# Two-layer hybrid decoder trunk: gMLP's v product first, norms by token halves, gate products one branch ahead, and the order of the last expert blocks

## The reference

```
h = rmsnorm(x, attn_norm_gain)
q, k, v, pz, gu, gv, g = split(h @ w_in)
gates = sigmoid(g + b_gate)                       # 3 branches x 1024
ya = sliding_window_attention(q, k, v, sinks, rel_bias) @ w_branch_a
yb = multiscale_pool(pz, w_pool, pool_scale) @ w_branch_b
yc = (gelu(gu) * spatial(rmsnorm(gelu(gv), v_gain))) @ w_branch_c
x = x + (gates[0]*ya + gates[1]*yb + gates[2]*yc) @ w_out
h2 = rmsnorm(x, ffn_norm_gain)
x = x + peer(h2)      # 8 heads, product keys, top 16 of 128*128 experts, gelu(h2 @ u) * gate @ v
```

## Time and profile before

| | us |
|---|---|
| median of 3 runs | 2060.33 |
| lowest and highest | 2059.02, 2060.73 |
| the profiled execution | 2059.37 |
| its span | 2057.6 |
| TensorE busy in it | 2017.3 |

### The profile page before, as it was taken

The page is one execution under the profiler, slowest core; times in us unless marked ns, Lnnn a source line. Parts: engine busy times, 40 slices in busy tenths (PEclk is TensorE's granted clock), DMA queues, the critical chain, the costliest instruction groups (busy, mean ns, idle before and its releaser), DMA issues.

```text
span 2057.6 us, 41405 instructions
## 1 busy us (share of the span) xinstructions
PE 2017.3 (98%) x13730; PEld 1874.1 (91%) x13730; DVE 1469.7 (71%) x2984; ACT 1057.9 (51%) x1751; POOL 1028.4 (50%) x427
## 2 busy tenths in 40 slices
PE   7999999999999999999989999999999999999997
PEld 6999899999998888889889999999999988888896
DVE  3943169688887888886649341796888778888775
ACT  5644454577774333334365444546777733333343
POOL 5798679877770000004368886797777600000042
PEclk9999999999999999999999999999999999999999
DMA  7455557665667777876454554576565677787763
GB/s 260 135 185 185 173 180 228 223 199 194 196 198 227 242 240 241 242 242 218 162 186 144 187 188 169 187 229 217 195 199 195 195 238 241 241 242 240 233 215 122
DMA packets 164486, 423.36 MB, mean 206 GB/s; under 512 B 18075, under 2 KB 76620, under 8 KB 163868
## 3 DMA queue, kind: packets, MB, share of 16 engines
q1 hardware_dynamic: 163724, 418.24, 63.3%
...
...
## 4 chain that ended last, share of the span: by engine, by line
PE 93%; issue 2%; POOL 2%; ACT 1%; DVE 1%; DMA 0%; DVEq 0%; POOLq 0%; ACTq 0%
PE bank L1112 53%; PE bank L1313 34%; PE bank L1364 3%; POOL halves L463 2%; PE bank L1291 1%; DVE hT L792 0%; PE bank L1274 0%; PE bank L1134 0%; PE bank L1213 0%; ACT area L505 0%; DMA x<-in_x 0%; ACT halves L528 0%; DVE area L785 0%; ACT area L559 0%; PE bank L1223 0%
## 5 line engine op out<-in xcount | busy, mean ns | idle before, releaser
L463 POOL TENSOR_TENSOR halves<-ring,halves 128x1024 fp32r<-128x1024 f32 x412 | 1021.8, 2490 | 992.7 <-DVE coef L1045 617.7
L528 ACT ACTIVATE halves<-ring 128x1024 fp32r<-128x1024 f32 x668 | 705.3, 1057 | 759.5 <-PE bank L1313 408.2
L1112 PE MATMUL bank<-hT,halves 128*128 128x256 f32 x8736 | 1081.5, 283 | 10.2 <-DVE hT L792 9.3
L1112 PEld LDWEIGHTS bank<-hT,halves 128*128 128x128 f32 x8736 | 1063.8, 192 | 16.2 <-DVE hT L792 10.8
L1313 PE MATMUL bank<-halves,coef 128*128 128x512 f32 x3072 | 703.0, 389 | 0.0
L1313 PEld LDWEIGHTS bank<-halves,coef 128*128 128x128 f32 x3072 | 574.4, 188 | 118.6 <-issue 0.5
L1027 DVE TENSOR_TENSOR halves<-ring,halves 128x1024 fp32r<-128x1024 f32 x256 | 315.8, 1234 | 10.4 <-ACT halves L528 10.0
L1039 DVE TENSOR_TENSOR act<-act,area 128x256 f32<-128x256 f32 x256 | 157.5, 615 | 58.8 <-ACT act L641 55.8
L1043 DVE CAST coef<-act 128x256 fp32r<-128x256 f32 x256 | 75.4, 294 | 100.8 <-PE bank L1313 98.0
L690 ACT ACTIVATE onehot<-onehot,weight 128x128 fp32r<-128x128 f32 x256 | 89.1, 395 | 108.2 <-DVE onehot L1010 108.1
L1004 DVE TENSOR_TENSOR onehot<-bank,ids 128x512 fp32r<-128x512 f32 x128 | 88.6, 692 | 48.5 <-PE bank L1364 48.5
...
## 6 DMA issues: line engine op xcount, KB each, us to landing
...
area<-rel_scratch SPq DMA_DIRECT2D x2, 1024.0 KB, 6.2
x_home<-x ACTq DMA_DIRECT2D x2, 1024.0 KB, 4.2
x<-x_home SPq DMA_DIRECT2D x2, 1024.0 KB, 8.0
rel_scratch<-act POOLq DMA_DIRECT2D x1, 1532.0 KB, 14.7
...
```

The lines of the kernel that those rows point to most:

```text
L463: pool.tensor_tensor(halves[:, s, 1, :], ring[:, s, :], halves[:, s, 0, :].bitcast(F32), ALU.subtract)\
L528: a.activation(halves[:, s, 0, :], ring[:, s, :], ACT.Copy).then_inc(hi_done, 1)
L1112: i = pe.matmul(o, stationary[a], moving[b], start=begin and n == 0, stop=end and n == len(TERMS) - 1)
```

## The change

Six things are done together.

1. The entry of a layer. x comes in two token halves on two queues; the parameters (`par`) come by a transfer of their own and not by the stream; SyncE, and no longer GpSimd, writes the relative bias rows out. The norm is made for one token half (`normed`): VectorE writes x times root times gain, TensorE transposes that against the identity, ScalarE and VectorE take high and low sides from PSUM. At layer 0 two matmuls spread the gain row over the partitions.
2. gMLP's v product, four tiles, follows the norm directly and goes by token halves; its gelu, root and scaling follow it. The triangle product of GpSimd now stands behind the low side of tile 19.
3. The four gate tiles of branch n + 1 come ahead of the two tiles of branch n (`MIX`), those of branch 0 before the attention transposes.
4. The output projection finishes token half 0 first, and the second norm goes by halves. Five matmuls that nothing reads (`KEEPERS`) replace four identity matmuls of 512 columns.
5. The last u block of a layer moves ahead of v block 125, and the last three v blocks go by token halves, so that half 0 is added to x and normed while half 1 is multiplied.
6. The final norm goes by halves with a gain that was loaded before, and the output is written in four transfers. Banks are allotted anew for this order.

```diff
+MIX = [("gate", 0)] + [step for n in range(2 * BR - 1) for step in (("gate", n + 1), ("branch", n))] + [("branch", 2 * BR - 1)]
+T_GATE, T_BRANCH = ([T_MIX + sum(4 if kind == "gate" else 2 for kind, _ in MIX[:MIX.index((name, n))])
+                     for n in range(2 * BR)] for name in ("gate", "branch"))
...
+    + [("lg1", "V")] * 4 + [("pz", "V")] * 2 + [("gu", "A")] * 2 + [("gate", "A")] * 2
+    + [("pT0", "A")] * 2 + [("pT1", "A")] * 4 + [("attn", "A")] * 4 + [("gmlp", "V")] * 2 + [("pool", "V")] * 2
+    + [(kind, "A" if kind == "gate" else "V") for kind, _ in MIX[1:] for _ in range(2)]
+    + [("wo", "V")] * 3 + [("h2T", "V")] * 2 + [("wo", "V")] + [("h2T", "V")] * 2 + [("qq", "A")] * 8 + [("score", "A")] * 8
...
+                if l == 0:
+                    sp.dma_start(x[:, 0, :], x_in[0, 0:P, :]).then_inc(x_loaded[0], 16)
+                    load(2, 2, l)
+                    sp.dma_start(ids[:, :], consts_in[:, 0:2 * P]).then_inc(consts_loaded, 16)
+                    load(3, 3, l)
+                    sp.dma_start(oh, consts_in[0:BUCKETS + 1, K_OH:K_END]).then_inc(rel_loaded, 16)
+                    sp.dma_start(relx[0:BUCKETS, :], rel_in).then_inc(rel_loaded, 16)
+                    load(4, 0, l)
+                    load(5, 1, l)
+                    sp.wait_ge(rel_vector, 1)
+                    sp.dma_start(scratch.rearrange("h (r i) d -> (h r) i d", i=HEADS),
+                                 relv.unsqueeze(1).to_broadcast([P, HEADS, NDIST])).then_inc(rel_written, 16)
...
+                for s in range(2, RING):
                     sp.wait_ge(lo_pool, l * LOP + (s + 2))
                     load(RING + s, s, l)
+                if l == 0:
+                    for s in range(2):
+                        sp.wait_ge(lo_pool, l * LOP + RING + s + 2)
+                        load(2 * RING + s, s, l)
                 sp.wait_ge(rel_written, 16)
                 sp.dma_start(bias, bass.AP(scratch.tensor, P - 1, [[NDIST - 1, P], [P * NDIST, HEADS], [1, 2 * P]]))\
                     .then_inc(bias_loaded, 16)
-                with sp.Fori(2, T_PU // RING + 1) as r:
-                    for s in range(RING):
+                if l == 0:
+                    load_maps(l)
+                def load_early(r, begin=0):
...
             for l in range(DEPTH):
 
-                pool.wait_ge(params_ready, l + 1)
+                pool.wait_ge(hi_done, l * HIS + 1)
                 pool.sem_inc(lo_pool, 2)
-                low(2, 2, l)
+                subtract(2)
                 low(3, 3, l)
-
+                with pool.Fori(1, 5) as r:
+                    for s in range(RING):
+                        low(r * RING + s, s, l)
+
+                pool.wait_ge(params_loaded, l * 16 + 16)
                 pool.wait_ge(maps_loaded, l * 16 + 16)
                 for g in range(GROUPS):
                     i = pool.tensor_tensor(wsp[:, g, :], par[:, C_WSP + g * P:C_WSP + (g + 1) * P], tril, ALU.mult)
                 i.then_inc(wsp_ready, 1)
-                with pool.Fori(1, T_PV // RING) as r:
+                with pool.Fori(5, T_PV // RING) as r:
                     for s in range(RING):
...
+                def gates(n):
+
+                    if n >= 3:
+                        a.wait_ge(taken_v, l * NGV + taken_before(place("branch", 2 * (n - 2) + 1) + 1)[0])
+                    for k in range(2):
+                        high_up_to(T_GATE[n] + 2 * k + 1 + 3)
+                        b = group("gate")
+                        for c in range(2):
+                            hf, br = divmod(n, BR)
+                            col = C_BGATE + br * KD + hf * 4 + 2 * k + c
+                            i = a.activation(sig_of(n)[:, 2 * k + c, :], b[:, c * S:(c + 1) * S], ACT.Sigmoid,
+                                             bias=par[:, col:col + 1])
+                        i.then_inc(taken_a, 1)
+
+                gates(0)
                 for n in range(2):
                     b = group("pT0")
...
+                def normed(n, t, gain):
+                    rstd(n + t, 2 + t, 4 + t, 1)
+                    for c, cols in enumerate(COLS):
+                        v.scalar_tensor_tensor(hn[:, t, cols], x[:, t, cols], stat[:, 4 + t:5 + t], gain(c),
+                                               ALU.mult, ALU.mult).then_inc(hn_ready, 1)
+
...
+                def gate_rows(j, t):
+
+                    if j % 2 == 0:
+                        pe.wait_ge(taken_v, rows_ready("h1T", 2 * t + j // 2 + 1))
+                    w = tile(T_GV + j, 2)
+                    for k in range(2):
+                        rows = [hT[:, e, 2 * j + k, t * P:(t + 1) * P] for e in range(2)]
+                        one, i = product(bv[t][:, :], rows, (w[:, 0, k], w[:, 1, k]), j == 0 and k == 0, j == 3 and k == 1)
+                        if t == 1 and k == 0:
+                            one.then_inc(tiles_used, 1)
+                    if j == 3:
+                        i.then_inc(groups_done, 1)
+
+                gate_rows(0, 0)
+                gate_rows(1, 0)
+                transpose_rows("h1T", 0, 1)
+                gate_rows(2, 0)
+                for j in range(3):
+                    gate_rows(j, 1)
+                gate_rows(3, 0)
+                gate_rows(3, 1)
...
-                            if t == 0 and k == 0:
-                                one.then_inc(tiles_used, 1)
-                        if kq == 3:
-                            i.then_inc(groups_done, 1)
-
-                pe.wait_ge(taken_v, l * NGV + taken_before(first("h2T"))[0])
-                for t in range(TT):
-                    for hf in range(2):
-                        pe.matmul(acc[2 * t + hf][:, :], ident, x[:, t, hf * HALF_N:(hf + 1) * HALF_N], start=True,
-                                  stop=True)
-                pe.wait_ge(diag_ready, l * 2 + 2)
-                transpose_rows("h2T")
-                pe.wait_ge(scaled, l * 4 + 3)
+                        projected(n, t, t == 0)
+                pe.wait_ge(merged_ready, l * 4 + 4)
+                for n in range(4, 8):
+                    tile(T_WO + n, 2)
+                    projected(n, 0, n == 4)
+                for n in range(4, 7):
+                    projected(n, 1, n > 4)
+                transpose_rows("h2T", 4, 0)
+                projected(7, 1, True)
+                for n in range(KEEPERS):
+                    pe.matmul(bank[7][:, 0:S], ident, ids[:, :], start=True, stop=True)
+                transpose_rows("h2T", 4, 1)
+                g[0] = first("qq")
...
+                def v_half(s, factors, t):
+
+                    for a, e in TERMS:
+                        for hf in range(2):
+                            i = pe.matmul(acc[2 * t + hf][:, :], factors[:, a, t * P:(t + 1) * P],
+                                          halves[:, s, e, hf * HALF_N:(hf + 1) * HALF_N], start=False, stop=True,
+                                          skip_group_check=True)
+                    return i
+
+                pe.wait_ge(lo_vector, l * LOV + NK - 1)
+                pe.wait_ge(coef_ready, l * NK + NK - 2)
+                v_half(0, coef[:, 1], 0)
+                pe.wait_ge(lo_pool, l * LOP + (NK - 1) + (T_PV - EARLY + 2))
+                pe.wait_ge(coef_ready, l * NK + NK - 1)
+                v_half(1, coef[:, 0], 0)
+                pe.wait_ge(lo_vector, l * LOV + NK + 1)
+                pe.wait_ge(coef_ready, l * NK + NK)
+                v_half(3, coef_last, 0).then_inc(acc_done, 1)
+                v_half(3, coef_last, 1).then_inc(tiles_used, 1)
+                v_half(0, coef[:, 1], 1).then_inc(tiles_used, 1)
+                v_half(1, coef[:, 0], 1).then_inc(tiles_used, 1)
 
```

605 lines of the change are left out of this document (341 added, 264 removed).

## The result

The changed kernel takes **2080.78 us** (median of 4, 2077.42 to 2083.48) against 2059.82 for the kernel before (2059.02 to 2060.73): 1.0101 times as long, 95% interval 1.0083 to 1.0118. Forecast was 2059.5, between 2050 and 2066. In the profiled executions the span went from 2057.6 to 2079.2 us, so there are 21.6 us to account for.

A forecast was written before the change was run, and what follows sets the result against it. TensorE, busy 2017.3 of 2057.6 us, was taken to bound the kernel. Terms 3.4 + 9.5 + 2.8 + 1.4 - 5.9 - 10.4 = 0.8 gave 2058.6, stated as a 2059.5 median, range 2050 to 2066.

The forecast's parts named there:

- GpSimd before the first gates: Behind the logits: moved triangle products and earlier exponentials add 3.0 us of wait a layer, 5.9 lost for two layers.
- The second norm: Projection to query columns: 8.1 us lost in place of 9.5, a gain of 1.4 a layer, 2.8 in all.
- merged wait: Fifth projection tile: TensorE newly waits 1.9 us for all four merged pieces.
- rival (c): Slower: the clock falls in the new waits, 13 us more at most, half giving 2066; chance 0.04.
- rival (b): Slower: VectorE's norm pieces collide with low sides, 13 us at most, half giving 2066; chance 0.09.
- The entry: Kernel start: halved x gains 2.9 us, less 1.5 of queue waits, so a gain of 1.4, bounds -4 and 4.
- queue waits: Entry, SyncE's queue: bias write and parameters ahead of tile loads cost 1.5 us, up to 6.
- bias write: Entry: 1532 KB written from SyncE's queue, taking 7.6 us without added waits, or 14.7 as in the kernel before.
- The gates: Gates 3, 4 and 5: ScalarE's wait for the sig slot delays tiles by 1.7 to 1.9 us, 5.2 lost a layer.
- From layer to layer: Boundary between layers: 5.1 us lost in place of 14.6, a gain of 9.5, bounds 7 and 11.
- the wait for tile 4: Between layers: tile 4's high side comes only behind half 1's root, a new TensorE wait of 1.4 us.
- The end: After TensorE's last product: 8.0 us in place of 11.4, a gain of 3.4, bounds 3 and 4.5.

The follow-up runs named there:

- Experiment 2: Changed kernel with GpSimd waiting for the second maxima before the low side of tile 15: 2080.72 us, ratio 1.0097 to the kernel before.
- 4: Changed kernel with high sides up to tiles 16 and 18 ahead of the exponentials and triangle products behind tile 23: 2064.56 us, 1.0022 to the kernel before.
- 1: Changed kernel with high sides of tiles 15 to 18, not only 15 and 16, made before the second exponentials: 2079.17 us, 1.0094 to the kernel before.
- 3: Changed kernel with high sides up to tiles 16 and 18 ahead of the two blocks of exponentials, as before: 2076.35 us, 1.0079 to the kernel before.
- 5: Changed kernel with only the triangle products moved, behind the low side of tile 23: 2080.67 us, 1.0100 to the kernel before.
- 8: Changed kernel with the last four projection tiles reordered, each waiting only for its own part of merged: 2076.08 us, 1.0073 to the kernel before.
- experiment 9: Changed kernel with the third query tile's high side made behind token half 1's transposed rows: 2075.02 us, 1.0073 to the kernel before.
- experiment 7: Changed kernel with SyncE's layer 0 queue reordered: tile 6 before the bias write, parameters and maps behind tiles 10 and 11: 2078.99 us, 1.0095 to the kernel before.

## Why the prediction was wrong

**What failed: "GpSimd before the first gates", 2.95 a layer where 8.2 was measured.** The step priced the triangle products at 2.63 and the earlier exponentials at 1.5 and took off what GpSimd had in hand. It had seen that the second exponentials begin ahead of a high side, but it treated that as delay on one engine. What it lacked is the return path: GpSimd's idleness ahead of the exponentials puts its next low sides on VectorE's second maxima, those hold up the exponentials, and these hold up the high sides that GpSimd needs. Experiment 2 shows the first link, 4 that undoing both moves gives all 8.9 back, and 1, 2, 3 and 5 that working on one delay alone gives 0.6 to 3.8. Of the 8.9 in layer 0, 7.0 are waits (5.65 and 1.31), 1.6 is the slow clock behind the first (10.50 for 8.89), the rest restarts. Nor does the sum of two prices hold for two delays in a row on one engine: 0.8 and 3.4 apart, 8.9 together.

**"The second norm", a gain of 1.4 where 2.2 was lost, in each layer.** The merged wait was foreseen and came as 2.51 for 1.9. In layer 0, 33.7 stand against the forecast's 21.95 + 8.1 = 30.1. Of the 3.6 between them 0.6 is the merged wait; 1.6 is a slow clock behind it (42 products in 11.43, in layer 1 in 9.86), rival (c); and the chain behind the last half tile took 241.20 - 234.52 = 6.7 for 5.2, since the second piece of half 1's norm met the third query tile's low side, rival (b). Experiments 8 and 9 take away the first and the last. In layer 1 the clock stayed up, and in place of the 1.6 stand 1.30 of waiting on half 0's norm, whose second piece met the first query tile's low side. VectorE and GpSimd, first in layer 0, then in layer 1:

```profile
230.57 1.42 DVE L919 SCALAR_TENSOR_TENSOR area<-x,stat,area 128x512 f32<-128x512 f32 x2
231.28 5.29 POOL L526 TENSOR_TENSOR halves<-ring,halves 128x1024 fp32r<-128x1024 f32 x2 [6.14 <-ACT halves L608]
```

```profile
1255.55 3.62 DVE L919 SCALAR_TENSOR_TENSOR area<-x,stat,area 128x512 f32<-128x512 f32 x2
1256.24 5.18 POOL L526 TENSOR_TENSOR halves<-ring,halves 128x1024 fp32r<-128x1024 f32 x2 [4.54 <-ACT halves L608]
```

The low side begins 0.71 after the first piece in the one and 0.69 in the other, just where the second piece begins; for half 1, late in both layers, it is 0.68. So a few hundredths of a microsecond seem to decide whether that piece takes 0.7 or 2.9; no experiment moved them alone.

**"The entry", a gain of 1.4 where 2.2 was lost.** The queue waits were put at 1.5 and are 3.2 (experiment 7), inside their bound of 6. The bias write took 11.2 from issue to landing, between the 7.6 and the 14.7 of the working. The rest is the other half of the term: without these waits the entry wins 1.0 and not 2.9. Of that, 1.3 is that v starts at 15.69 and not at 14.4: its first low side is ready at 14.76, and the bias product (1.64) stands in between. Behind that the working foresaw 2 us of waiting for tile 4; TensorE has no idle row there, but v's first twelve products took 5.40, where twelve took 3.06 in layer 1, at a granted clock of 1.00 in both, and no run shows why. By the Trainium skill (page "SBUF — State Buffer", section "SBUF: two separate sides"), as the prediction read it, a write from SyncE's queue is not held up by VectorE, and the prediction put it near 7.6. The trace does not decide it: the write took 11.2, and four ring tiles shared the DMA engines with it.

**What held.** The gates: 4.4 of waits and 5.3 in all a layer for 5.2, at gates 3, 4 and 5, at the second tile, behind VectorE's taking; gate 4 was no worse than the others, since the halving stands behind the taking. From layer to layer: 9.7 for 9.5, v 2.6 after the last v block's end for 2.65, the wait for tile 4 1.32 for 1.4. The end: half 1's adds begin at 2072.37, 0.5 behind TensorE's last product (2069.09 + 12 x 0.2275), and the span ends 7.4 after that product, a gain of 4.0 for 3.4; the last row of the table shows 1.2 less, since it also holds 1.0 of slow clock behind the norm of layer 1; experiment 9, without it, has 810.37 there for 811.38.

**The rivals.** (b) and (c) had 0.09 and 0.04 and were priced as ends of their own. Both happened in part, on top of the forecast terms: 1.3 for half 1's piece in each layer and 1.3 for half 0's in layer 1, 1.6 and 2.0 for the clock at tile 17 (72 products in 10.50 and 10.90), 1.6 at the norm of layer 0. Against (b) the prediction said that ScalarE has only just begun the high side then. That was so each time: it began 0.42 to 0.44 ahead of the first piece. But a high side takes 1.06, and the second piece begins 0.7 behind the first, so the low side arrives just with the second piece; the argument covers the first one only. Of the port of VectorE and GpSimd the Trainium skill (page "SBUF — State Buffer", section "SBUF: two separate sides") says that the engine that starts first has it for the whole instruction and the other blocks fully. The traces agree: a piece is 0.7 or 2.9, an operation on 8 columns 0.17 or, just behind the start of a low side, 2.0 to 2.4, and 0.47 where 0.44 of a low side was left. By that rule the length of the VectorE operation does not matter, only whether it starts beside a low side; the prediction had asked it of 512-column pieces only.
